# Shared-expert products and products of constants put into TensorE's waits

## The chip, the cores and the metric

One core of one Trainium2 chip runs the whole program in one launch. The metric is the device time of that launch in microseconds. Everything is float32.

## The reference, cut to what matters

Two layers (`DEPTH = 2`) of a diffusion backbone over 256 context and 256 latent tokens, width 1024. Layer 0 works on all 512 tokens (four tiles of 128), layer 1 writes only the 256 latent ones (two tiles).

```
for l in range(DEPTH):
    mod = silu(c) @ w_mod[l] + b_mod[l]
    h   = modulate(rms_norm(x), mod[0], mod[1])
    mix = gated delta rule | latent attention | windowed GQA | dense GQA of (h @ w_in[l])
    x   = x + mod[2] * (mix @ w_out[l])
    h   = modulate(rms_norm(x), mod[3], mod[4])
    x   = x + mod[5] * moe_ffn(h)

def moe_ffn(h):                      # 64 experts, 6 of them for each token
    scores = sigmoid(h @ router_w)
    idx    = top_k(scores + router_bias, 6)
    gates  = scores[idx] / sum(scores[idx]) * 2.5
    # assignments sorted by expert, each expert: swiglu of width 384
    return sum over k of gates[k] * swiglu(h, expert idx[k]) + swiglu(h, shared)
```

## The kernel before, in words

The engines run their own programs and meet at semaphores. A layer goes through stages. Input projections end with a barrier of all engines. The **delta rule** runs over four blocks (`b`) of 128 tokens in two directions (`d`): per block TensorE makes the decays (`decays`, L1153 and L1159) and the products of keys (`products`), then a long chain of small 64x64 products (`blocks`, L1142) in turn with ScalarE and VectorE. Its first block needs GpSimd's `X` (L2474) and then, for the step "n2", VectorE's transposed tile "NT" (L2081). Attention and the output projection (L1349) follow.

The **expert stage** starts with a sorting. Routing scores give a mask (VectorE, ends at L2272). TensorE sums it into positions (`positions`, L1380 and L1382). VectorE makes a key per expert, compares keys (`beats`, L2286), finds the first eight experts (`sorted_round(0)`, which releases the first weight loads, `sorted_ready` 1), then needs the ranks from TensorE (`ranks`, L1388; copied at L2311), and makes one-hot rows for slots (L2328) which TensorE multiplies into the lists by expert (`lists_by_expert`, L1394) and by unit (`lists_by_unit`, L1399). The finished lists (L2333 to L2336) release GpSimd's gathers of token rows (L2566). Then VectorE runs the seven other sorting rounds (L2290 to L2298); the last one gives `sorted_ready` 2, on which all later expert weights wait.

Work on tokens goes by units, n = 0, 1, 2, ... Units 0 and 1 (`EARLY = 2`) are two tiles of the shared expert, which need no gather and whose weights are loaded before the sorting; the others are routed experts, with the last shared tiles (layer 0 only) late among them. A unit is `unit_part(n, "lo")` and `unit_part(n, "hi")` (gate and up products, L1479, eight k-steps in two halves), SiLU on ScalarE (L1796), `unit_times` on VectorE (L2254), `act_transposed` (L1495, copied at L1802), `unit_down` (L1504), and copies out: ScalarE L1817 and VectorE L2260 (`shared_out`) or L2409. Routed tokens are transposed by `unit_transposed` (L1461) and copied by `unit_copied` (L2392, L2393).

Weights move in chunks of 1536 KB through a ring of eight slots (`SLOTS = 8`); the queue of SP issues them in the order of use (L890). The first three chunks are the shared expert's, the next five belong to units 2 and 3 and are the ones released by `sorted_ready` 1. Each later chunk waits until the chunk before it in its slot was used: after the lo half (`lo_used`), the hi half (`gu_psum`) or the down products (`down_psum`). For the ninth chunk and the two behind it these are unit 1's lo, hi and, in layer 0, down.

TensorE's order around the sorting is written out by hand, separately for `n_t == 4` (layer 0) and `n_t == 2` (layer 1):

```
layer 0: unit 0 hi | positions | act 0 | down 0 | ranks | unit 1 lo, hi | lists | act 1 | down 1 | unit 2 transposed
layer 1: unit 0 hi | positions | act 0 | down 0 | ranks | lists | unit 1 lo, hi | unit 2 transposed
```

After the units comes the **combining** (`combined`, one function per engine). Rows of expert outputs are read back by token (`yrow`, L934, 3072 KB a tile). GpSimd makes a diagonal of the gates (L2628, `diag_ready`), TensorE multiplies diagonals with rows (L1007; the trace shows each float32 product as two MATMULs, so a tile is 20 of them), VectorE adds and scales (L1920 to L1922, `resid_ready`). In layer 0 the next layer's norm follows tile by tile (VectorE L1905 to L1907, `normed_tile` on TensorE, L1021), then a barrier and the next layer's convolution projections (L1037). In layer 1 the output store follows and the program ends.

## Time and profile before

| what | value |
|---|---|
| time, median of 3 runs | 2623.26 us (2618.08 to 2626.28) |
| the profiled execution's own time | 2640.14 us |
| its span, first to last instruction | 2638.3 us, 41374 instructions |
| TensorE busy | 2256.7 us (86%), mean granted clock 0.944 |
| VectorE, ScalarE, GpSimd busy | 730.8 us (28%), 425.1 us (16%), 311.4 us (12%) |
| DMA queue of SP | 740.46 MB, 68.1% of 16 engines' span |
| expert weights | 256 + 128 loads of 1536 KB |

A timeline row gives the start, the length from first start to last end, engine, line, operation, output and inputs, one shape, the count, and in brackets the idle time before it with what ended it. The stages of layer 0 lie at about 196 to 305 us (delta rule), 544 to 594 (sorting), 594 to 1390 (units), 1396 to 1453 (combining and norm); those of layer 1 at 1586 to 1690, 1802 to 1840, 1840 to 2598 and 2603 to the end.

### The profile page before, as it was taken

The page shows a single profiled execution, that of the slowest core. Times are in us where ns is not written, and L with a number is a line of the kernel's source. Part 1 is how long each engine was busy: PE and PEld are TensorE (multiplying, and loading weights), DVE is VectorE, ACT ScalarE, POOL GpSimd, SP SyncE. Part 2 cuts the span into 40 slices and gives each one's busy share as a digit, 9 for nine tenths or more (in the row PEclk, how much of TensorE's full clock was granted, in tenths as well). Part 3 has the DMA queues.
Part 4 walks back from the last instruction along what each step waited for, and adds up shares of the span by engine and source line. Part 5 has one row for each costly group of instructions (what it writes and reads, how often), then busy time and mean ns, then how long its engine had stood idle before and what let it go on. Part 6 is the DMA issues. An engine that isn't in the chain of part 4 may idle for free. (4 is left out here: it accounts for less than half of the span.)

```text
span 2638.3 us, 41374 instructions
## 1 busy us (share of the span) xinstructions
PE 2256.7 (86%) x17495; PEld 1168.1 (44%) x17495; DVE 730.8 (28%) x1621; ACT 425.1 (16%) x886; POOL 311.4 (12%) x368
## 2 busy tenths in 40 slices
PE   6998899989877887888896998898978879888886
PEld 2457644454333343344443557755433334343332
DVE  3465554363101110111114365555211011111111
ACT  2323443210000000000001232441000000000000
POOL 0007200011111111110000006200111110000000
PEclk9999997999999999999998999999999999999998
DMA  7000286349999999999997010125999999999994
GB/s 321 32 18 33 102 356 262 127 163 389 426 422 416 410 416 421 410 421 398 381 397 324 33 41 19 70 101 218 351 426 418 413 417 420 420 415 416 414 421 182
DMA packets 96349, 780.99 MB, mean 296 GB/s; under 512 B 21736, under 2 KB 22136, under 8 KB 37280
## 3 DMA queue, kind: packets, MB, share of 16 engines
q1 hardware_dynamic: 74848, 740.46, 68.1%
q0 software_dynamic: 21312, 37.81, 3.8%
q8 instruction: 143, 2.34, 0.3%
q14 instruction: 46, 0.38, 0.0%
HBM read 772.55 MB, written 41.29 MB: 308 GB/s over the span
## 5 line engine op out<-in xcount | busy, mean ns | idle before, releaser
L1479 PE MATMUL banks<-arena,htreg 128*32 128x384 f32 (+2 forms) x5824 | 870.7, 529 | 218.0 <-DMA arena<-in_exp_w_gu 212.7
L1479 PEld LDWEIGHTS banks<-arena,htreg 128*32 128x32 f32 (+2 forms) x5824 | 401.5, 136 | 660.3 <-issue 511.3
L1504 PE MATMUL banks<-arena,modreg 128*32 128x512 f32 (+2 forms) x2184 | 398.2, 596 | 28.9 <-issue 25.5
L2254 DVE TENSOR_TENSOR modreg<-modreg,banks 128x384 f32<-128x384 f32 x74 | 41.0, 554 | 1044.3 <-ACT modreg L1796 1040.6
L1504 PEld LDWEIGHTS banks<-arena,modreg 128*32 128x32 f32 (+2 forms) x2184 | 134.2, 127 | 240.1 <-issue 236.3
L1049 PE MATMUL banks<-arena,htreg 128*128 128x512 f32 (+3 forms) x480 | 158.9, 490 | 0.0
L2409 DVE COPY modreg<-banks 128x512 f32<-128x512 f32 x68 | 47.0, 692 | 304.4 <-PE banks L1504 304.4
L1796 ACT ACTIVATE modreg<-banks 128x384 f32<-128x384 f32 x74 | 36.4, 492 | 541.7 <-PE banks L1479 541.7
L1802 ACT ACTIVATE modreg<-banks 128x384 f32<-128x384 f32 x74 | 36.3, 491 | 520.8 <-PE banks L1495 520.8
L2572 POOL DMA_INDIRECT y_d<-modreg,lst x68 | 67.5, 993 | 441.6 <-DVE modreg L2409 440.7
L1049 PEld LDWEIGHTS banks<-arena,htreg 128*128 128x128 f32 x480 | 89.6, 191 | 64.9 <-issue 60.9
L1817 ACT ACTIVATE modreg<-banks 128x512 f32<-128x512 f32 x68 | 40.6, 597 | 424.2 <-PE banks L1504 424.2
L2566 POOL DMA_INDIRECT htreg<-h_d,lsg x34 | 35.0, 1031 | 528.8 <-PE banks L1461 498.6
L2566 POOL DMA_INDIRECT hreg<-h_d,lsg x34 | 35.0, 1030 | 520.5 <-PE banks L1461 453.8
L1007 PE MATMUL banks<-arena 128*128 128x512 f32 x120 | 57.3, 638 | 31.6 <-DMA arena<-y_d 31.6
L1349 PE MATMUL banks<-arena,htreg 128*128 128x512 f32 x192 | 83.2, 593 | 0.0
L1304 PE MATMUL banks<-arena 64*128 64x512 f32 (+3 forms) x144 | 78.5, 630 | 2.6 <-ACT arena L1730 2.6
L1037 PE MATMUL banks<-htreg,arena 128*128 128x512 f32 (+1 forms) x192 | 78.7, 574 | 1.2 <-ACTq L703 0.7
L1142 PE MATMUL banks<-arena 64*64 64x64 f32 x1536 | 59.7, 226 | 7.5 <-DVE arena L2081 6.8
L1142 PEld LDWEIGHTS banks<-arena 64*64 64x64 f32 x1536 | 52.5, 140 | 15.4 <-DVE arena L2081 8.1
L959 PE MATMUL banks<-arena,crep 128*32 128x512 f32 x256 | 41.2, 733 | 20.2 <-DMA arena<-in_w_mod 20.2
L1314 PEld LDWEIGHTS banks<-const,htreg 128*128 128x128 f32 x240 | 28.4, 154 | 64.5 <-issue 42.4
(398 smaller groups left out, 2186.4 us busy)
## 6 DMA issues: line engine op xcount, KB each, us to landing
arena<-in_exp_w_gu SPq DMA_DIRECT2D x256, 1536.0 KB
arena<-in_exp_w_down SPq DMA_DIRECT2D x128, 1536.0 KB
arena<-in_w_mod SPq DMA_DIRECT2D x32, 1024.0 KB, 9.4
arena<-y_d SPq DMA_DIRECT2D x6, 3072.0 KB, 16.7
modreg<-in_w_mod SPq DMA_DIRECT2D x14, 1024.0 KB, 7.9
modreg<-mod_d SPq DMA_DIRECT2D x20, 512.0 KB
arena<-in_shared_w_gu SPq DMA_DIRECT2D x6, 1536.0 KB
arena<-in_w_in SPq DMA_DIRECT2D x4, 2048.0 KB, 12.9
```

The lines of the kernel that those rows point to most:

```text
L959: last = mm(bank[32 * c_:32 * c_ + 32, :], crep[:, k, :], w[:, 512 * c_:512 * c_ + 512], start=(k == 0), stop=(k == KD - 1))
L1007: last = mm(ps[4 + 2 * (i % 2) + half][:], diag[i % 2][:, k, :], yrow[i % YB][:, k, 512 * half:512 * half + 512], start=(k == 0), stop=(k ...
L1037: last = mm(qkv_bank(ct)[:, lo:], win_qkv[:, k, tok(ct)], hT[:, k, lo:], start=(i == 0), stop=(i == KD - 1))
L1049: last = mm(ps[2 + n % 4][:, lo:w], hT[:, k, tok(t)], win[g][:, k, lo:w], start=(k == 0), stop=(k == KD - 1))
L1142: last = mm(out[r, at + HALF * g:at + HALF * g + HALF], lhs(r, g), rhs(r, g), start=True, stop=True)
L1304: mm(ps[s % 2][:, 0:nk * P], q_, k_, start=True, stop=True).then_inc(scores_psum.sem, 1)
L1349: last = mm(ps[2 + n % 2][:], mixT[:, k, tok(t)], wout[:, k, 512 * half:512 * half + 512], start=(k == 0), stop=(k == KD - 1))
L1479: last = mm(gu_bank(n, half)[rows, 0:DE], src[:, k, rows], up4[q][:, i, DE * half:DE * (half + 1)], start=(k == 0), stop=(k == KD - 1))
L1504: last = mm(ps[4 + half][rows, :], actT[:, k, rows], dn3[q][:, k, 512 * half:512 * half + 512], start=(k == 0), stop=(k == KE - 1))
L2409: dve.tensor_copy(outs[r % 2][:, 512:1024], ps[5][:]).then_inc(unit_y.sem, 1)
L2566: pool.indirect_dma_start(out=slots[l][r % 2], out_offset=None, in_=h_d, in_offset=bass.IndirectOffsetOnAxis(ap=lsg1[:, u:u + 1], axis=0), ...
L2572: pool.indirect_dma_start(out=y_d, out_offset=bass.IndirectOffsetOnAxis(ap=lst1[:, u:u + 1], axis=0), in_=outs[r % 2], in_offset=None, bou ...
```

## The change

`keep_warm` multiplies the identity with 512 columns of constants into a bank that nothing reads; it is called in four places on TensorE. TensorE's order in the sorting becomes:

```
layer 0: unit 0 hi | unit 1 lo | positions | act 0 | ranks | down 0 | unit 1 hi | lists | act 1 | down 1 | unit 2 transposed
layer 1: unit 0 hi | positions | act 0 | down 0 | ranks | unit 1 lo | lists by expert, by unit | unit 1 hi | unit 2 transposed
```

On VectorE, in layer 0, `shared_out(0)` moves from ahead of the ranks, and `unit_times(1)` from behind the lists, to a place between the last one-hot row and the lists; `unit_copied(EARLY)` goes ahead of `shared_out(1)`. Nothing else changes.

```
@@ -949,6 +949,11 @@
         @block.tensor
         def _(pe):
             mm = pe.matmul
+
+            def keep_warm(bank, n):
+                for _ in range(n):
+                    mm(bank, ident, const[:, 0:512], start=True, stop=True)
+
             pe.wait_ge(ident_loaded.sem, 16)
             pe.wait_ge(cond_silu.sem, 1)
             pe.transpose(ps[4][:, 0:2 * KD], crow, ident[0:2 * KD, 0:2 * KD]).then_inc(first_psum.sem, 1)
@@ -999,6 +1004,8 @@
                 for i in range(NOUT[l] + 1):
                     if i < NOUT[l]:
                         pe.wait_ge(diag_ready.sem, diag_ready.at(l, i + 1))
+                        if i == 0:
+                            keep_warm(ps[4], 8)
                         pe.wait_ge(yrow_loaded[i % YB].sem, yrow_loaded[i % YB].at(l, i // YB + 1))
                         if i >= 2:
                             pe.wait_ge(resid_ready.sem, resid_ready.at(2 * l + 1, i - 1))
@@ -1007,6 +1014,9 @@
                                 last = mm(ps[4 + 2 * (i % 2) + half][:], diag[i % 2][:, k, :],
                                           yrow[i % YB][:, k, 512 * half:512 * half + 512], start=(k == 0), stop=(k == BY_PE - 1))
                             last.then_inc(out_psum.sem, 1)
+                    if i == NOUT[l] and l + 1 < DEPTH:
+                        pe.wait_ge(resid_ready.sem, resid_ready.at(2 * l + 1, i - 1))
+                        keep_warm(ps[4], 6)
                     if i and l + 1 < DEPTH:
                         normed_tile(2 * (l + 1), i - 1)
 
@@ -1180,8 +1190,10 @@
                                               start=True, stop=True)
                         pe_.done(last, l, b, "kk")
 
+                keep_warm(delta[0].C, 1)
                 decays(0)
                 products(0)
+                keep_warm(delta[0].C, 2)
                 both = list(zip((0, 1), delta, g_pe, g_act, g_dve, g_pool))
                 for b in range(NB):
                     for d, D_, pe_, act_d, dve_, pool_ in both:
@@ -1522,16 +1534,18 @@
                     act_transposed(0)
                     unit_down(0)
                     ranks()
+                    unit_part(1, "lo")
                     lists_by_expert()
                     lists_by_unit()
-                    unit_up(1)
+                    unit_part(1, "hi")
                     unit_transposed(EARLY)
                 else:
+                    unit_part(1, "lo")
                     positions()
                     act_transposed(0)
+                    ranks()
                     unit_down(0)
-                    ranks()
-                    unit_up(1)
+                    unit_part(1, "hi")
                     lists_by_expert()
                     lists_by_unit()
                     act_transposed(1)
@@ -2305,8 +2319,6 @@
                 link(ts(latecol[lo64], rankcol[lo64], float(NE - G_), -float(NE - U_), ALU.is_ge, ALU.mult))
                 link(ts(rankcol[lo64], rankcol[lo64], dropcol[lo64], latecol[lo64], ALU.add, ALU.add))
                 link(ts(unit_hot[lo64, 0:U_], K("experts")[lo64, 0:U_], rankcol[lo64], None, ALU.is_equal))
-                if n_t > 2:
-                    shared_out(0)
                 dve.wait_ge(rank_psum.sem, rank_psum.at(l, 1))
                 link(dve.tensor_copy(rank, ps[0][:, 0:NE]))
                 link(ts(shift_by, rank, float(U_), 2.0, ALU.is_ge, ALU.mult))
@@ -2329,6 +2341,9 @@
                        ).then_inc(slot_hot_ready.sem, 1)
                 dve.wait_ge(slot_hot_used.sem, slot_hot_used.at(l, TOPK * n_t))
                 dve.tensor_copy(listT, ps[1][lo64, 0:P]).then_inc(listT_ready.sem, 1)
+                if n_t > 2:
+                    shared_out(0)
+                    unit_times(1)
                 dve.wait_ge(list_psum.sem, list_psum.at(l, 1))
                 link(ts(row64[:, 0:U_], ps[0][:, 0:U_], 0.0, float(NO_CODE), ALU.is_equal, ALU.mult))
                 link(stt(row64[:, 0:U_], ps[0][:, 0:U_], -1.0, row64[:, 0:U_], ALU.add, ALU.add))
@@ -2336,8 +2351,6 @@
                 ts(lsg1[:, 0:U_], lst1[:, 0:U_], 3, None, ALU.logical_shift_right).then_inc(lists_ready.sem, 1)
                 if n_t == 2:
                     shared_out(0)
-                else:
-                    unit_times(1)
                 for j in range(1, NE // 8):
                     sorted_round(j)
                 if n_t == 2:
@@ -2392,11 +2405,9 @@
                     dve.tensor_copy(hgT[q % 2][:, 0:4, :], ps[0][:].rearrange("p (k n) -> p k n", k=4))
                     dve.tensor_copy(hgT[q % 2][:, 4:8, :], ps[1][:].rearrange("p (k n) -> p k n", k=4)).then_inc(slotT.sem, 1)
 
-                if n_t == 2:
-                    unit_copied(EARLY)
-                else:
+                unit_copied(EARLY)
+                if n_t > 2:
                     shared_out(1)
-                    unit_copied(EARLY)
                 gates_made()
                 def unit_out(n):
                     if is_shared(l, n):
```

## Rows read from the trace of the kernel before

**Rows 1.** Windows; columns: us, PE, PEld, DVE, ACT, POOL busy, PEclk, DMA share, GB/s.

```profile
580.00:590.00 10.00, 7.54 (x37) 4.46 (x37) 8.32 (x44) 0.49 (x1) 2.04 (x2) 1.00 0.51 182
...
640.00:700.00 60.00, 52.21 (x537) 21.69 (x539) 7.56 (x12) 4.74 (x9) 8.96 (x9) 0.97 1.01 426
...
1833.00:1890.00 57.00, 55.47 (x282) 29.79 (x281) 17.77 (x47) 4.63 (x9) 6.02 (x6) 1.00 0.82 300
```

**Rows 2.** Timeline of TensorE, layer 0's sorting; start us, us, what, xcount [idle before].

```profile
555.52 1.44 PE L1380 MATMUL banks<-arena,const 128*128 128x320 f32 x2 [3.96 <-DVE arena L2272]
556.75 2.45 PE L1382 MATMUL banks<-arena,const 128*128 128x256 f32 x8
...
566.19 10.59 PE L1479 MATMUL banks<-arena,htreg 128*128 128x384 f32 x32
576.70 6.17 PE L1394 MATMUL banks<-arena,modreg 128*64 128x128 f32 x48
...
586.36 5.39 PE L1504 MATMUL banks<-arena,modreg 128*128 128x512 f32 x12 [0.67 <-ACT modreg L1802]
...
594.01 10.59 PE L1479 MATMUL banks<-arena,htreg 128*128 128x384 f32 x32 [1.38 <-DVE htreg L2393]
```

**Rows 3.** Timeline of VectorE, the same stretch.

```profile
560.72 0.25 DVE L2286 TENSOR_SCALAR stat<-arena,stat 64x64 f32<-64x64 f32 x1
...
565.99 0.69 DVE L2260 COPY hreg<-banks 128x512 f32<-128x512 f32 x1 [2.78 <-PE banks L1504]
566.60 0.21 DVE L2311 COPY arena<-banks 128x64 f32<-128x64 f32 x1
...
574.18 1.11 DVE L2328 TENSOR_SCALAR arena<-const,arena 128x128 f32<-128x128 f32 x4
```

**Rows 4.** Timeline of the weight loads' queue, the same stretch.

```profile
592.27 7.68 SPq L890 DMA_DIRECT2D arena<-in_exp_w_gu  x4
```

**Rows 5.** Timeline of TensorE, layer 1's sorting.

```profile
1820.79 5.38 PE L1394 MATMUL banks<-arena,modreg 128*64 128x128 f32 x24 [5.34 <-DVE arena L2328]
...
1826.98 10.59 PE L1479 MATMUL banks<-arena,htreg 128*128 128x384 f32 x32
...
1839.99 5.43 PE L1479 MATMUL banks<-arena,htreg 128*128 128x384 f32 x16 [1.53 <-DVE htreg L2393]
```

**Rows 6.** Timeline of GpSimd, layer 1's first gather.

```profile
1828.80 1.08 POOL L2566 DMA_INDIRECT hreg<-h_d,lsg  x1 [66.41 <-DVE lsg L2336]
```

**Rows 7.** Timeline of GpSimd, the diagonals of layers 0 and 1.

```profile
1396.50 2.47 POOL L2628 TENSOR_TENSOR arena<-const,gate 128x640 f32<-128x640 f32 x2 [4.01 <-issue]
...
2602.96 2.47 POOL L2628 TENSOR_TENSOR arena<-const,gate 128x640 f32<-128x640 f32 x2 [2.90 <-issue]
```

**Rows 8.** Timeline of TensorE, both combining stages and what follows layer 0's.

```profile
1406.38 19.38 PE L1007 MATMUL banks<-arena 128*128 128x512 f32 x40 [16.39 <-DMA arena<-y_d]
...
1453.49 1.97 PE L1021 MATMUL banks<-const,hreg 128*128 128x128 f32 x8 [7.24 <-DVE hreg L1907]
...
1456.17 37.29 PE L1037 MATMUL banks<-htreg,arena 128*128 128x256 f32 x96 [0.72 <-ACTq L703]
...
2612.82 20.32 PE L1007 MATMUL banks<-arena 128*128 128x512 f32 x40 [15.25 <-DMA arena<-y_d]
```

**Rows 9.** Windows while the combining starts, columns as in rows 1.

```profile
1410.00:1412.00 2.00, 2.00 (x6) 0.97 (x5) 0.00 (x0) 0.00 (x0) 0.00 (x0) 0.91 1.14 492
...
2618.00:2620.00 2.00, 2.00 (x5) 0.91 (x4) 0.00 (x0) 0.00 (x0) 0.00 (x0) 0.83 0.46 197
```

**Rows 10.** Timeline of TensorE, first delta block of layers 0 and 1.

```profile
206.59 1.15 PE L1142 MATMUL banks<-arena 64*64 64x64 f32 x32 [2.52 <-DVE arena L2081]
...
213.27 1.08 PE L1153 MATMUL banks<-arena,const 128*64 128x256 f32 x8
...
1593.96 1.40 PE L1142 MATMUL banks<-arena 64*64 64x64 f32 x32 [2.36 <-DVE arena L2081]
...
1602.19 1.08 PE L1153 MATMUL banks<-arena,const 128*64 128x256 f32 x8
```

31 lines of the change are left out of this document (20 added, 11 removed).

## The prediction

> **What bounds the kernel now.** I read the windows of the page's slices first, then the timelines of each engine around the places that the change touches. The windows show two kinds of stretches. While units run, the DMA engines are full: share 1.01 at 426 GB/s with TensorE busy for 52 of 60 us [rows 1]. The expert weights set the pace there, and a change in that stretch would bring nothing. Ahead of it DMA is not full: share 0.51 in the last part of layer 0's sorting, and still 0.82 over the first 57 us of units in layer 1, where TensorE is busy 55.5 of 57 us and hands back slots of the ring too late [rows 1]. So what counts is when the stream of weights becomes continuous, and what starts it earlier moves everything behind it. Two things start it: the last sorting round, on which the ninth chunk waits (issued at 592.27 [rows 4]), and the start of unit 2, whose halves free further slots (594.01 [rows 2] and 1839.99 [rows 5]).
>
> **Term A, layer 0's sorting.** TensorE stands idle for 3.96 us up to 555.52, waiting for the mask [rows 2]. Unit 1's lo half, 16 MATMULs of the 32 that take 10.59, so 5.3 us [rows 2], now runs from 551.6 to 556.8. That makes positions start 1.3 later. But they ran at the low clock: 10 MATMULs from 555.52 to 559.20, 3.7 us, for 1920 columns in all; the pace of unit 1 (10.59 for 32 x 384 columns, 0.86 ns a column [rows 2]) gives 1.65, and with 0.4 for ends 2.05. Behind an unbroken run I expect the high clock, so positions end at 558.85, 0.35 earlier than before. If the clock fell anyway they would end 1.3 later.
> Next, ranks needs VectorE's comparison, before complete at 560.97 [rows 3], now 560.6. It no longer stands behind unit 0's down products. Before, VectorE waited 2.78 us for these (until 565.99), copied their output for 0.69, and took the ranks at 566.60 [rows 3]. Now it reaches them at 565.99 - 2.78 - 0.3 = 562.9, 3.7 earlier, and its first one-hot row moves from 574.18 [rows 3] to 570.5. TensorE does ranks until 561.0, down 0 in 5.3 until 566.3, and hi in 5.3 until 571.6. So the lists start at 571.6 instead of 576.70 [rows 2], 5.1 earlier; TensorE is what is late here, and VectorE's one-hot rows stand ready.
> Behind the last one-hot row VectorE now does the shared copy (0.69) and unit 1's product (0.55 by the same columns); about 0.5 of that lies in its wait for the lists by unit, and the product was ahead of the seven rounds before as well. The ninth chunk moves by 5.1 + 0.5 - 0.7 = 4.9, to 587.4. Down 1 was at 586.36 [rows 2]; its input is ready at 579.3, with transpose and copy it starts near 580.6 and ends at 585.9. It frees a slot ahead of 587.4. Unit 2's transposes follow, then VectorE's two copies (1.3), and unit 2 starts at 588.2, 5.8 earlier. Slots that unit 2 frees come 5.8 earlier, the first chunk 4.9: I take **5.3**. Bounds: 3.5, if the positions are 1.3 late and VectorE's added work of 1.2 shows in full (5.3 - 1.6 - 0.2), and 5.8.
>
> **Term B, layer 1's sorting.** Here ranks stays where it was. TensorE sits idle for 5.34 us ahead of 1820.79, in which the clock falls: 24 MATMULs of the lists take 5.38 (0.224 each), against 48 in 6.17 (0.129 each) in layer 0 [rows 2, 5]. Unit 1's lo half, 5.3, fits into the 5.34. It delays nothing, and the lists then take 12 x 0.257 = 3.1: 2.3 gained. Only hi remains behind them (TensorE was busy with both halves for 10.59 from 1826.98 [rows 5]), so it ends at 1824.6 + 5.3 = 1829.8 instead of 1837.5. What is late next is the gather of unit 2's rows: it was issued at 1828.80 [rows 6], now 1826.5. How long it takes cannot be read, since it was covered; it is under 1837.4 - 1828.8 = 8.6. The other late part is VectorE: seven rounds from 1826.2, some 6.1 us, unit 1's product, then the two copies. With about 5 for the gather both sides meet near 1832.5 to 1833, and unit 2 starts at 1834.4, against 1839.99 [rows 5]: 5.6. With 8.6 for the gather it starts at 1837.5: 2.5. The ninth chunk itself moves only 2.3, but DMA has 0.18 x 57 = 10 us of slack in the stretch [rows 1], so unit 2's start counts. I take **5.3**, bounds 2.3 and 5.9.
> The Trainium skill, "DMA: Bandwidth & Descriptors", section "Anatomy of one DMA", gives a fixed 2.0 us for a DMA of GpSimd plus its bytes at 436 GB/s. For 512 KB that would be 3.2 us by an estimate from this page, the gather would be there before the hi half ends, and term B would be about 5.8.
>
> **Term C, 8 constant products ahead of each combining.** Each is two MATMULs of 512 columns: 0.44 us at the pace of rows 2, 0.88 at half clock. Their room is from the first diagonal (1396.50 + 1.25 and 2602.96 + 1.25 [rows 7]) to the rows' arrival (1406.38 and 2612.82 [rows 8]): 8.6 us in both layers. Queued behind them are the combining products, and behind those VectorE. The clock rose 4.0 us after the first product in layer 0 (share at the high level in the window from 1410) and 5.9 after it in layer 1 [rows 8, 9]. So 16 MATMULs take between 9.0 (4.6 cold, 11.4 warm) and 10.0 (6.7 cold, 9.3 warm), mean 9.5: 0.9 late. What they save: 40 MATMULs took 19.38 and 20.32 [rows 8] against 40 x 0.44 = 17.6, so 1.8 and 2.7. Net **0.9** and **1.8**. Bounds: 0.4 to 1.4 and 1.3 to 2.3, and -5.5 each if the clock stayed low throughout (16 x 0.88 = 14.1 in 8.6).
>
> **Term D, 6 constant products ahead of layer 0's last tile.** TensorE is idle 7.24 us there [rows 8]; 12 x 0.44 = 5.3 fit in. The wait on the residual that is added ahead of them is for tile 2, which VectorE has done by then. The eight transposes take 1.97 and would take half, and the 96 MATMULs behind them take 37.29 [rows 8] for 80 x 0.44 = 35.2 at full clock. Together **3.0** if the clock holds over the remaining 2 us of idle time, 0 if it does not.
>
> **Term E, constants in the delta rule.** One product ahead of the first decays costs 0.9 in a wait of 1.7 for GpSimd: nothing. Two products, 1.8 us, lie in the waits of 2.52 (layer 0) and 2.36 (layer 1) [rows 10], nothing. In layer 0 the clock held; from first product to the next block's decays took 213.27 - 206.59 = 6.7. In layer 1 it took 1602.19 - 1593.96 = 8.2 [rows 10]. Gain **1.5** in layer 1, bounds 0 and 1.5. Were a cover gone, 1.8 a layer would show.
>
> **Sum.** 5.3 + 5.3 + 0.9 + 1.8 + 3.0 + 1.5 = 17.8 us. The profiled execution took 2640.1 (span 2638.3), 16.9 above the median of 2623.3; I take the same 17.8 off the median: **2605.5 us**. The Trainium skill, "TensorE: Matmul & The Clock Gate", section "Part 1: The HAM clock gate", says that the number of cold products varies from run to run of one kernel. By that, terms C to E would differ between executions within the bounds above, and the sum with them.
>
> **The rivals.** (1) The forecast, 0.66. (2) The early start is partly given back: the gather, and VectorE's rounds behind it, hold unit 2 back in both layers, and one of D and E fails. 3.5 + 2.3 + 2.7 + 3.0 = 11.5, 2612. For it: the gather's time isn't seen. Against it: layer 0's gather is issued 4.9 ahead of its use, and the rounds end before it. 0.17. (3) The stream does not begin earlier in effect: later slots are freed by units whose pace is set elsewhere, and DMA's slack closes. Only C, D and E remain, 7.2: 2616. For it: in layer 1 DMA reaches full share only after some 50 us. Against it: TensorE is without pause there, so an earlier start has to carry through. 0.09. (4) The clock doesn't rise during constant products, as if the change did not do what it says: C gives -11, D and E nothing, A and B 9.3 (A without the positions' gain 4.0): 2625. Against it: products of this shape raise it in both layers [rows 9]. 0.04. (5) Slower: the gathers and chunks now overlap more, and the weight stream loses rate. 302 MB a layer at 426 GB/s take 709 us, so 1% costs 7.1 a layer; from 1.8% in both layers it decides (25.6), at 2.3% it gives 2605.5 + 32.6 = 2638. For it: layer 1's first 57 us show only 300 GB/s [rows 1]; against it: these are waits for slots, not a low rate. 0.04.
>
> **Numbers.** A measurement of this kernel can tell about 0.3%, 7.9 us, from no change. Faster by more: (1) and nearly all of (2), 0.82. Within: (3), (4) and the rest, 0.14. Slower 0.04. The upper bounds sum to 5.8 + 5.9 + 1.4 + 2.3 + 3.0 + 1.5 = 19.9, and 5 more for the spread of the three runs: 2598. The other end takes in (2) and half of (3): 2616.
>
> **What would show it.** Right: the lists of layer 0 start about 5 us after TensorE's mask wait than before relative to it, that is 20 instead of 25 us after unit 0's hi half; the ninth chunk is issued 4.9 earlier, unit 2 of layer 1 starts 5.6 earlier against ranks; the 40 combining MATMULs take 17.6 and start about 0.9 behind their rows; clock 1.00 at L1037 and after L1142's first product. Wrong: a new wait for a gather at L1461, a wait of TensorE for weights in the first units, or a weight stream that ends no earlier although it began earlier.

## The result, and the profile after

| | time | ratio to the kernel before, 95% interval |
|---|---|---|
| kernel after | 2609.25 us (2605.43 to 2622.77, 14 runs) | 0.9934 (0.9919 to 0.995) |
| kernel before, beside it | 2626.78 us (2618.08 to 2633.53, 14 runs) | |
| kernel after, timed again with later experiments | 2611.6 us (2605.08 to 2622.28, 6 runs) | 0.9937 (0.9915 to 0.9958) |

17.5 us less, where 17.8 were forecast. The profiled execution of after took 2607.57 us (span 2605.8). The two profiled spans differ by 32.5 us, which is more than the medians do. 10.4 of it lie between the delta rule's last decays and unit 0's hi half of layer 0, in attention, which the change does not touch. That stretch alone took between 261 and 281 us in the fourteen profiled executions of this study. So spans of whole executions are not compared here; stages are. Below, a row or tile is called cold where it ran at the low clock. Lines of a kernel shift with each edit; L955 is the products of constants.

Layer 0's sorting on TensorE (rows 2 has the same stretch of before; columns: start us, length, engine, line, operation, output and inputs, count, idle time before it and what ended it):

```profile
535.58 10.59 PE L1491 MATMUL banks<-arena,htreg 128*128 128x384 f32 x32
546.00 0.70 PE L1392 MATMUL banks<-arena,const 128*128 128x320 f32 x2
546.54 1.31 PE L1394 MATMUL banks<-arena,const 128*128 128x256 f32 x8
...
549.68 0.43 PE L1400 MATMUL banks<-stat,const 64*128 64x64 f32 x2 [1.45 <-DVE stat L2300]
550.04 5.42 PE L1516 MATMUL banks<-arena,modreg 128*128 128x512 f32 x12
555.29 5.33 PE L1491 MATMUL banks<-arena,htreg 128*128 128x384 f32 x16
560.55 6.17 PE L1406 MATMUL banks<-arena,modreg 128*64 128x128 f32 x48
...
569.45 7.08 PE L1516 MATMUL banks<-arena,modreg 128*128 128x512 f32 x12 [0.67 <-ACT modreg L1816]
...
578.87 10.59 PE L1491 MATMUL banks<-arena,htreg 128*128 128x384 f32 x32 [1.45 <-DVE htreg L2406]
```

Positions and the idle time ahead of them read as forecast: no wait for the mask, 0.70 and 1.31 us at full clock instead of 1.44 and 2.45 [rows 2]. Lists start 25.0 us behind the start of unit 0's hi half, before 30.6 (19.6 and 25.1 behind its end, where the prediction had 20 and 25). New is the length of unit 1's down products, 7.08 us for the 12 MATMULs that took 5.39 [rows 2]. SP issued the ninth chunk at 576.11 (40.5 us behind the hi half, before 46.1), and the windows of after say what happened to the clock while the down products ran (columns: busy us and count of each engine, granted clock, DMA share, GB/s):

```profile
576.11 1.37 SPq L890 DMA_DIRECT2D arena<-in_exp_w_gu  x3
```

```profile
570.00:572.00 2.00, 2.00 (x4) 0.76 (x3) 1.79 (x12) 0.00 (x0) 1.69 (x2) 0.61 1.00 334
572.00:574.00 2.00, 2.00 (x4) 0.93 (x3) 1.76 (x12) 0.00 (x0) 0.03 (x1) 0.54 0.84 277
```

Behind the lists' small products and three waits of 0.38 to 0.67 us the granted clock is 0.61 and 0.54, in the middle of large products with TensorE busy throughout. The same rows and waits left it at 1.00 in another execution (e1 below), so they do not explain the fall by themselves.

Layer 1's sorting, TensorE and GpSimd of after (against rows 5 and 6):

```profile
1787.87 5.43 PE L1491 MATMUL banks<-arena,htreg 128*128 128x384 f32 x16
1793.28 3.25 PE L1406 MATMUL banks<-arena,modreg 128*64 128x128 f32 x24
...
1797.24 5.43 PE L1491 MATMUL banks<-arena,htreg 128*128 128x384 f32 x16
1805.60 1.68 PE L1473 MATMUL banks<-const,hreg 128*128 128x128 f32 x8 [2.93 <-DMA hreg<-h_d,lsg]
1808.66 7.51 PE L1491 MATMUL banks<-arena,htreg 128*128 128x384 f32 x16 [1.38 <-DVE htreg L2406]
```

```profile
1799.06 1.08 POOL L2577 DMA_INDIRECT hreg<-h_d,lsg  x1 [64.20 <-DVE lsg L2351]
```

The lists take 3.25 instead of 5.38 us, as forecast. Then TensorE waits 2.93 us for the gather, which took 6.5 us from its issue. The wait costs a second time: the granted clock is still 1.00 from 1804 to 1806, then 0.51 and 0.50 up to 1812, and unit 2's first half takes 7.51 us instead of 5.4.

Combining, the last tile's constants and transposes, the projections (L1047) and the delta rule of layer 1, TensorE (against rows 8 and 10):

```profile
1381.18 9.62 PE L955 MATMUL banks<-const 128*128 128x512 f32 x16 [7.78 <-POOL arena L2639]
1390.64 17.33 PE L1014 MATMUL banks<-arena 128*128 128x512 f32 x40
...
1410.13 8.82 PE L1014 MATMUL banks<-arena 128*128 128x512 f32 x20 [1.29 <-POOL arena L2639]
...
1429.12 5.32 PE L955 MATMUL banks<-const 128*128 128x512 f32 x12
1435.69 1.09 PE L1031 MATMUL banks<-const,hreg 128*128 128x128 f32 x8 [1.25 <-DVE hreg L1921]
1437.56 36.24 PE L1047 MATMUL banks<-htreg,arena 128*128 128x256 f32 x96 [0.77 <-ACTq L703]
```

```profile
1572.43 1.15 PE L1152 MATMUL banks<-arena 64*64 64x64 f32 x32 [0.53 <-DVE arena L2095]
...
1579.11 1.08 PE L1163 MATMUL banks<-arena,const 128*64 128x256 f32 x8
...
2583.13 17.43 PE L1014 MATMUL banks<-arena 128*128 128x512 f32 x40 [0.57 <-DMA arena<-y_d]
```

40 combining MATMULs take 17.33 and 17.43 us instead of 19.38 and 20.32. In layer 0 the constants end behind their rows (no idle time ahead of the combining), in layer 1 0.57 us before them. TensorE's third tile starts within 0.1 us of the landing of its own rows in both kernels, 30.1 and 30.3 us behind the first diagonal; what reaches the projections goes through VectorE, whose adding of the second tile starts 1.2 us earlier behind the first diagonal.

Stage by stage, in us, for all profiled executions. *hi-u2*: unit 0's hi half to unit 2's start in layer 0. *u2-dg*: on to the first diagonal. *dg-pr*: on to the projections L1047. *pr-dc*: on to layer 1's first decays. *dc*: on to the next block's decays. *dc-rk*: on to the ranks. *rk-u2*, *u2-dg*, *dg-end*: the same for layer 1, from its ranks to unit 2, to the first diagonal and to the end.

```
                          hi-u2  u2-dg  dg-pr  pr-dc    dc  dc-rk  rk-u2  u2-dg  dg-end
before                     47.9  802.5   59.7  131.1  14.9  212.8   25.0  763.0    35.3
e11_combining_constants    51.6  802.4   58.3  128.6  15.7  209.9   24.9  762.7    32.9
e10_delta_constants        48.5  802.9   59.4  129.4  13.4  209.2   24.9  763.3    35.0
e2_constants_only          51.0  803.2   57.8  128.2  13.4  208.4   25.0  761.9    33.5
e4_layer1_order            51.4  800.1   59.3  129.4  15.8  209.9   21.1  763.9    35.1
e3_layer0_order            44.8  802.4   59.8  131.1  14.9  213.0   24.9  761.9    34.2
e5_copy_before_ranks       47.6  800.1   59.5  131.0  14.9  213.2   24.9  763.0    35.2
e1_order_only              41.6  801.9   59.7  131.3  14.9  213.0   21.6  765.1    34.2
after                      43.3  801.0   57.7  128.1  13.4  208.4   21.2  763.5    33.7
e17_after_again            43.3  802.9   58.1  128.4  13.4  207.9   20.9  764.8    33.4
e14_six                    43.3  803.1   58.9  126.8  13.4  208.1   20.7  764.1    33.6
e15_last_chunk             43.3  801.2   57.6  131.3  13.4  208.0   19.1  764.9    33.5
e12_five_more              41.7  802.4   57.9  128.5  13.4  211.1   21.0  763.3    32.9
e16_rounds                 41.7  805.1   58.3  129.2  13.4  208.4   20.6  762.9    33.1
```

### The profile page after: what moved, and what is told of

Its sections match the earlier page's. It is cut to its first block and busy times, and to the rows that moved or that the text cites. A ratio compares the mean times of both kernels' runs of the same rounds, so it can differ in the third digit from the quotient of the medians.

```text
span 2605.8 us, 41483 instructions
## 1 busy us (share of the span) xinstructions
PE 2265.0 (87%) x17551; PEld 1163.8 (45%) x17551; DVE 729.3 (28%) x1621; ACT 423.8 (16%) x886; POOL 311.1 (12%) x368
## 5 line engine op out<-in xcount | busy, mean ns | idle before, releaser
L1059 PEld LDWEIGHTS banks<-arena,htreg 128*128 128x128 f32 x480 | 89.4, 190 | 64.6 <-issue 60.7
L1047 PE MATMUL banks<-htreg,arena 128*128 128x512 f32 (+1 forms) x192 | 77.7, 568 | 1.2 <-ACTq L703 0.8
L1316 PE MATMUL banks<-arena 64*128 64x512 f32 (+3 forms) x144 | 71.3, 577 | 3.3 <-ACT arena L1744 3.3
L1361 PEld LDWEIGHTS banks<-arena,htreg 128*128 128x128 f32 x192 | 36.2, 190 | 44.0 <-issue 44.0
L1047 PEld LDWEIGHTS banks<-htreg,arena 128*128 128x128 f32 x192 | 37.5, 196 | 40.2 <-issue 37.2
```

Source lines behind the costliest of these rows:

```text
L1047: last = mm(qkv_bank(ct)[:, lo:], win_qkv[:, k, tok(ct)], hT[:, k, lo:], start=(i == 0), stop=(i == KD - 1))
L1059: last = mm(ps[2 + n % 4][:, lo:w], hT[:, k, tok(t)], win[g][:, k, lo:w], start=(k == 0), stop=(k == KD - 1))
L1316: mm(ps[s % 2][:, 0:nk * P], q_, k_, start=True, stop=True).then_inc(scores_psum.sem, 1)
L1361: last = mm(ps[2 + n % 2][:], mixT[:, k, tok(t)], wout[:, k, 512 * half:512 * half + 512], start=(k == 0), stop=(k == KD - 1))
```

## The experiments

My theory was the forecast's: orders (A, B) and constants (C, D, E) each give their part. The rivals: it is all one of the two, or the weight stream takes the early start back. A gain in us below is the ratio's distance from 1 times 2630 us. The medians give somewhat other gains: 12.1 us for e1, 10.8 for e2, 10.1 for e3, 4.3 for e4, 4.6 for e10, 20.6 for e12.

### Orders alone and constants alone

e1_order_only deletes the four sets of constants, e2_constants_only keeps them and puts back both sorting orders and VectorE's steps.

```
e1:  -                        if i == 0:
     -                            keep_warm(ps[4], 8)
     ...
     -                keep_warm(delta[0].C, 2)
e2:  -                    unit_part(1, "lo")
                          positions()
                          act_transposed(0)
     -                    ranks()
                          unit_down(0)
     -                    unit_part(1, "hi")
     +                    ranks()
     +                    unit_up(1)
     ...
```

> All constant products are taken out; both new orders of the sorting and VectorE's moved steps stay. Theory (the forecast's terms A and B are real, C to E come on top): 8.4 to 10.6 us faster than the kernel before (8.4 by the stage lengths of the two profiled executions, 4.6 in layer 0 and 3.8 in layer 1; 10.6 by the forecast), so about 0.9965 of it, and the combining again takes 19 to 20 us for its 40 MATMULs. Rival (the whole gain is clock, the earlier start of the weight stream is lost again in the units): within 3 us of the kernel before, with unit 2 to the diagonal longer by what the sorting won. Rival (only the orders count): 15 us or more faster.

> The four sets of constant products alone, on the orders of before. Theory: 6 to 8 us faster than the kernel before: combining 1 in layer 0 and 1.8 in layer 1, last tile and decays 3, layer 1's delta rule 1.5; with e1_order_only's gain it sums to the whole 17.5. Rival (only the orders count): within 2 us of the kernel before. Rival (the clock, kept higher at these places, also avoids the low stretches elsewhere): over 10 us faster, and more in stretches without a constant product.

Measured beside each other: e1 2617.87 us, ratio 0.9951 (0.9931 to 0.9971), 12.9 us faster (0.0049 x 2630). e2 2619.16 us, 0.9964 (0.9944 to 0.9983), 9.5 us faster. e1 is not within 3 us of before and e2 is not within 2 us, so both rivals of the kind "only one counts" fall. Together they make 22.4, against the 17.5 of the whole; each has an interval of about 5 us to both sides, which holds the difference. The combining of e1 took 19.58 and 19.27 us, as expected. The time does not exclude e2's last rival, over 10 us with a gain in stretches without a constant, and the stages bear it out in part: *dc-rk* has no constant in it and was 4.4 us shorter than in before.

### One layer's order at a time

e3_layer0_order_only is e1 with layer 1's order put back, e4_layer1_order_only is e1 with layer 0's.

```
e3:  -                    unit_part(1, "lo")        e4: as in the diff of e2,
                          lists_by_expert()             TensorE and VectorE of layer 0
                          lists_by_unit()
     -                    unit_part(1, "hi")
     +                    unit_up(1)
```

> Layer 0's order of TensorE and VectorE alone; no constant product, layer 1 as before. Theory: 4.6 us faster by the stage lengths (5.3 by the forecast): ninth chunk 5 to 5.6 us earlier against unit 0's hi half, unit 2 4.6 to 5.8 earlier, all of it carried to the diagonal. Down 1 again takes about 7 us and not 5.4, if the clock falls behind the small products of the lists. Rival (stream gives it back): under 2 us, and layer 0's units longer by the same amount.

> Layer 1's order of TensorE alone (unit 1's lo half between ranks and lists). Theory: 3.8 us faster by the stage lengths (5.3 by the forecast), with TensorE idle about 3 us for the gather of unit 2's rows ahead of its transposes, and the gather landing about 6.5 us after its issue. Rival (DMA's slack in layer 1's first units closes and only the ninth chunk counts): 2.3 us or less, units of layer 1 longer by the rest. Sum of e3 and e4 should be e1 within 2 us.

Measured: e3 2619.85 us, 0.9975 (0.9956 to 0.9994), 6.6 us faster. e4 2625.63 us, 0.9994 (0.9977 to 1.0011), 1.6 us faster, not to be told from nothing. Their sum is 8.2, e1 had 12.9; each has intervals of 5, so the 2 us that I had expected them to agree within could not be tested. Nor do the times exclude the rivals, under 2 us for e3 and 2.3 or less for e4; for e3 the stages do, since *u2-dg* (802.4) is that of before.

The stages say more than the times. In layer 0 the way to unit 2 depends on whether the clock falls in the two sets of down products. TensorE of e1, and of e3:

```profile
545.60 5.42 PE L1509 MATMUL banks<-arena,modreg 128*128 128x512 f32 x12
...
565.01 5.39 PE L1509 MATMUL banks<-arena,modreg 128*128 128x512 f32 x12 [0.67 <-ACT modreg L1809]
```

```profile
543.81 7.11 PE L1509 MATMUL banks<-arena,modreg 128*128 128x512 f32 x12
...
564.92 6.91 PE L1509 MATMUL banks<-arena,modreg 128*128 128x512 f32 x12 [0.67 <-ACT modreg L1808]
```

5.4 and 5.4 us in e1, 7.1 and 6.9 in e3, of the same code. The old order has both cases too: 5.39 twice in before and e10, 7.0 to 7.4 twice in e2, e4 and e11. So like must be held against like: with both sets at full clock 41.6 (e1) against 47.9 and 48.5 (before, e10), 6.3 and 6.9 less; with the fall in both 44.8 (e3) against 51.0, 51.4 and 51.6, 6.1 to 6.8 less. **Layer 0's order is worth 6.1 to 6.9 us** at unit 2's start, and the profiled pair showed 4.6 only because the clock fell in one set of after and in none of before.

In layer 1 the offsets to before, measured from the ranks, tell where the gain stays (start of each unit, in us against the same start in before):

```
unit        e3      after     e1      e12     e15     e16
2         -0.06    -3.81   -3.36   -3.93   -5.88   -4.32
3         -0.07    -1.76   -1.55   -3.94   -4.22   -4.32
6         -0.06    -1.75   -1.55   -3.94   -4.22   -4.32
8         -0.76    -2.97   -1.19   -4.26   -5.03   -4.19
20        -1.09    -3.41   -0.89   -3.67   -3.66   -3.85
35        -1.11    -3.32   -1.29   -3.58   -3.91   -4.42
```

In after unit 2 starts 3.8 us earlier, and unit 3 only 1.8: the 2.05 between are unit 2's cold first half (7.51 against 5.43). It is constant from there to unit 6, while TensorE alone sets the pace. Behind that the offsets move by 1 us and more, also in e3, which has layer 1 as before. In after the gain grows again, to 3.3 us at unit 35, so the 2.05 us lost ahead of unit 3 are not all missing at the end; e12 and e15, 2.2 and 2.5 us ahead of after at unit 3, are 0.3 and 0.6 ahead at unit 35.

At the first diagonal, counted from the ranks, the six executions with layer 1's old order have 786.8 to 788.2 us, mean 787.6, and the five that have the new order and no further change of layer 1's units (e1, e4, after, e14, e17) 784.7 to 786.7, mean 785.4. So **layer 1's order is worth about 2.2 us there**, with a spread of 1 us between executions of one kernel. e1, at 786.7, shows almost nothing of it.

### VectorE's part in layer 0

e5_layer0_copy_before_ranks takes e3 and puts the copy back ahead of the ranks:

```
+                if n_t > 2:
+                    shared_out(0)
                 dve.wait_ge(rank_psum.sem, rank_psum.at(l, 1))
...
                 if n_t > 2:
-                    shared_out(0)
                     unit_times(1)
```

> e3_layer0_order_only with one step put back: in layer 0 VectorE copies unit 0's down products before it takes the ranks, as in the kernel before; TensorE's order stays new. Theory (the ranks taken ahead of the copy are what lets the lists start early): VectorE waits for down 0 until about 20 us after unit 0's hi half and reaches its first one-hot row 7.6 us behind the ranks' copy, so TensorE's lists start 3 us later than in e3_layer0_order_only (about 28 to 29.5 us after unit 0's hi half instead of 25 to 26.7), TensorE waits for them, and unit 2 starts about 3 us later. Rival (TensorE alone is late, VectorE's order costs nothing): lists and unit 2 as in e3_layer0_order_only within 0.5 us.

Measured, one execution: 2624.69 us. VectorE and TensorE of e5:

```profile
555.29 0.69 DVE L2266 COPY hreg<-banks 128x512 f32<-128x512 f32 x1 [5.38 <-PE banks L1509]
```

```profile
563.88 7.54 PE L1399 MATMUL banks<-arena,modreg 128*64 128x128 f32 x48 [3.52 <-DVE arena L2334]
```

VectorE waits 5.38 us for the down products, and TensorE then waits 3.52 for VectorE's one-hot rows. The lists come 30.3 us behind unit 0's hi half, 5.3 later than in e1 and 3.6 later than in e3, and the rival falls. Its way to unit 2 (47.6) looks like that of before (47.9), but the two are not alike: in e5 the first down products took 7.11 us and the lists 7.54 instead of 6.2, the second down products 5.39. Against e3, with the 1.5 us that e3's second down products lost to the clock added, the copy's old place costs about 4.3 us, an estimate from one execution each. By the same reckoning (49.2 against 51.0 to 51.6) TensorE's new order alone still brings about 2 us, so VectorE's move is most of what layer 0's order is worth, and not all of it.

### What the constants do further on

In after and e2, with all constants, *dc-rk* was 208.4 us, in before, e1 and e3 212.8 to 213.0, and no constant product stands in this stretch. e10 keeps only the delta rule's three products, e11 only those at the combining.

```
e10: -                            keep_warm(ps[4], 8)      e11: -                keep_warm(delta[0].C, 1)
     -                        keep_warm(ps[4], 6)               -                keep_warm(delta[0].C, 2)
     (both: orders as in e2)
```

> Only the three constant products of the delta rule, everything else as before. Open: in the kernel after and in e2_constants_only the way from layer 1's second decays to its ranks took 208.4 us, in the kernel before, e1 and e3 212.9, with no constant product in it. Theory F (the delta rule's constants keep the clock in block 2 and leave it so that the two later low stretches do not fall): 208.4 us here too, and 13.4 instead of 14.9 between the first decays, 6 us faster than before in all. Rival G (the combining's constants, which only shift all later work against the clock's falls, do it): 212.9 us here, 1.5 us faster in all.

> Only the constant products ahead of the combining in both layers and ahead of layer 0's last tile. Theory F of e10_delta_constants_only: 212.9 us from layer 1's second decays to its ranks. Rival G: 208.4 us. Either way the diagonals to L1047's place is 2.0 us shorter and the way from there to the decays 2.9 shorter, and the end comes 1.7 us earlier against layer 1's first diagonal.

Measured: e10 2624.71 us, 0.9992 (0.9971 to 1.0013), an interval that holds both the 6 us of F and the 1.5 us of G; e11 2621.33 us in one execution. *dc-rk* was 209.2 in e10 and 209.9 in e11, and e4, without a constant, had 209.9 as well. Neither F nor G is right as put, and e4 shows that the stretch varies by 3 us by itself. Between before and after, two stretches of low clock differ (the first windows of 20 us are of before, the next of after, at the same places behind the second decays):

```profile
1602.20:1622.20 20.00, 17.49 (x460) 15.37 (x460) 11.57 (x31) 5.12 (x11) 11.96 (x18) 0.91 0.01 2
1702.20:1722.20 20.00, 19.21 (x145) 11.31 (x146) 9.69 (x29) 11.03 (x24) 0.00 (x0) 0.83 0.23 95
```

```profile
1579.10:1599.10 20.00, 17.49 (x514) 15.36 (x512) 12.00 (x32) 5.75 (x12) 13.50 (x21) 1.00 0.01 3
1679.10:1699.10 20.00, 18.70 (x183) 11.27 (x182) 12.48 (x40) 11.92 (x30) 0.00 (x0) 1.00 0.12 52
```

Six of seven executions with both kinds of constants had 207.9 to 208.4 (the seventh 211.1), four of five with neither had 212.8 to 213.2 (the fifth 209.9). The constants go with some 4 us here; by what path stays open. *dc* is plain: 13.4 in all eight with the delta rule's constants, 14.9 to 15.8 in all six without. Layer 0's first block, where the prediction saw nothing to gain, shows it too: from its first decays to the next block's it took 16.0 us in all eight, and in the six without 15.9 in three and 17.1 to 18.7 in the other three (e1, e3, e11).

### More constants

e12_five_more_constants fills three more waits of after:

```
 layer 1: unit_part(1, "hi")           layer 0: act_transposed(0)         layer 0: lists_by_unit()
         +keep_warm(ps[6], 3)                  +keep_warm(ps[6], 1)               +keep_warm(ps[6], 1)
          unit_transposed(EARLY)                ranks()                            act_transposed(1)
```

> The kernel after plus five more constant products: one ahead of layer 0's ranks (in the 1.45 us wait for VectorE), one ahead of the transposes for unit 1's down products, three in layer 1 between unit 1's hi half and the transposes of unit 2, where TensorE waits 2.9 us for the gather. Theory: the clock holds, unit 0's and unit 1's down products take 5.4 us each instead of up to 7.1, unit 2 of layer 0 starts 41.6 to 42.2 us after unit 0's hi half (43.3 in the kernel after), transposes in layer 1 take 1.05 instead of 1.7 and unit 2's lo half 5.4 instead of 7.5; 3 to 4 us faster than the kernel after, 20 to 22 faster than before. Rival: the added products only lengthen the path (0.9 us in layer 0) and the clock falls all the same: 0 to 1 us slower than the kernel after.

TensorE of e12, layer 0 and layer 1:

```profile
563.35 1.02 PE L955 MATMUL banks<-const 128*128 128x512 f32 x2
...
565.33 5.42 PE L1516 MATMUL banks<-arena,modreg 128*128 128x512 f32 x12
...
582.72 1.12 PE L955 MATMUL banks<-const 128*128 128x512 f32 x2
...
584.86 5.39 PE L1516 MATMUL banks<-arena,modreg 128*128 128x512 f32 x12 [0.67 <-ACT modreg L1819]
...
1820.91 2.74 PE L955 MATMUL banks<-const 128*128 128x512 f32 x6
1824.41 1.16 PE L1473 MATMUL banks<-const,hreg 128*128 128x128 f32 x8 [0.77 <-DMA hreg<-h_d,lsg]
1826.95 5.43 PE L1491 MATMUL banks<-arena,htreg 128*128 128x384 f32 x16 [1.38 <-DVE htreg L2409]
```

The stages came as expected: 41.7 us to unit 2 in layer 0, both sets of down products at 5.4, and in layer 1 unit 3 keeps 3.94 instead of 1.76 us. The time was 2608.71 us, 0.9902 (0.9878 to 0.9925), 25.8 us faster than before by the ratio and 20.6 by the medians. Against after's 0.9934 and 0.9937 the intervals overlap, so 3 to 4 us over after fit, but are not shown by the times. In layer 1 little of it reaches the first diagonal: 784.4 us behind the ranks, where after had 784.6, e14 784.8 and e17 785.7.

### The gather, and the number of constants

e15_last_chunk_after_gather holds one weight chunk back, e14_six_before_combining takes two products away.

```
e15: +                    if l == 1 and loaded == 7:
     +                        sp.wait_ge(gathered[0].sem, gathered[0].at(l, 1))
e14: -                            keep_warm(ps[4], 8)
     +                            keep_warm(ps[4], 6)
```

> The kernel after with one more wait on SP: in layer 1 the fifth of the chunks issued together (the last before the ninth chunk's round) is issued only when unit 2's rows are gathered. In the kernel after the gather was issued at 1799.06 and landed about 6.5 us later, with the DMA engines at share 1.0 for the first 4 of them. Theory (the gather is slow because it shares the DMA engines with the weight chunks issued ahead of it): 3 to 4 us from issue to landing, TensorE's wait ahead of unit 2's transposes falls from 2.9 us to under 1, the clock stays, and unit 2 starts 18 to 19 us behind ranks instead of 21.2. Rival (6.5 us is the gather's own time, or that of the scattered rows): the wait stays at about 2.9 us and unit 2 starts at 21.2 us. The units of layer 1 take no more than 1 us longer in either case.

> The kernel after with 6 instead of 8 constant products ahead of each combining. In layer 0 the 8 held the combining back by 0.9 us after its rows had come (the 16 MATMULs take 9.1 to 9.6 us, cold at first), in layer 1 they ended 0.6 us before. Theory: 12 MATMULs take 7.4 to 7.9 us, combining in layer 0 begins with its rows, 9.9 us behind the first diagonal instead of 10.8, and its 40 MATMULs still take 17.4 us, so 0.9 us gained in layer 0, nothing in layer 1. Rival (the clock falls again in the 1 to 1.5 us of idle time between them and the combining, or has not risen in one of the layers): the 40 MATMULs take 18.5 us or more in that layer, so slower than with 8.

GpSimd and TensorE of e15:

```profile
1802.65 1.08 POOL L2579 DMA_INDIRECT hreg<-h_d,lsg  x1 [64.20 <-DVE lsg L2353]
```

```profile
1807.16 1.16 PE L1475 MATMUL banks<-const,hreg 128*128 128x128 f32 x8 [0.90 <-DMA hreg<-h_d,lsg]
1810.19 7.10 PE L1493 MATMUL banks<-arena,htreg 128*128 128x384 f32 x16 [1.86 <-DVE htreg L2408]
```

4.5 us from issue to landing instead of 6.5 (6.5 to 7.0 in the seven executions with this order and no chunk held back), and TensorE's wait falls from 2.93 to 0.90: at least 2 us of the gather's time are spent behind the chunks. What the remaining 4.5 us are, with four chunks issued ahead, stays open; the theory had 3 to 4. Unit 2 starts 19.1 us behind the ranks, just outside the expected 18 to 19, but the clock still fell (7.10 us), against the theory, and of the 2.1 us won, 0.6 were left at the first diagonal (19.1 + 764.9 against 21.2 + 763.5), less than the 1.1 us between after and e17. One execution each: e15 2610.41 us, e14 2610.69, before beside them 2621.48.

e14's combining began with its rows, 10.0 us behind the first diagonal. But TensorE, being earlier, waited longer for the rows of the third tile, which landed 30.4 us behind the first diagonal, and that tile ran cold:

```profile
1393.22 17.43 PE L1014 MATMUL banks<-arena 128*128 128x512 f32 x40 [0.60 <-DMA arena<-y_d]
...
1413.64 10.52 PE L1014 MATMUL banks<-arena 128*128 128x512 f32 x20 [2.12 <-issue]
```

10.52 us for 20 MATMULs instead of 8.82, and 58.9 us from the diagonal to the projections instead of 57.7: slower in this stage, though by neither way that I had named. VectorE had been 0.6 us ahead of after, and then waited 1.62 us for the cold tile. The length of the wait alone does not decide: in e12 the same tile waited 2.20 us and ran at full clock, in 8.82 us. So what 6 products bring when the third tile stays fast is open.

The stage behind it gave the loss back: 126.8 us from the projections to the decays, after 128.1. The projections themselves took 34.64 us instead of 36.24, and their first 4 us ran at 1.00 in e14 (first fence) and at 0.59 in after (second):

```profile
1440.23 1.09 PE L1031 MATMUL banks<-const,hreg 128*128 128x128 f32 x8 [0.59 <-DVE hreg L1921]
1442.10 34.64 PE L1047 MATMUL banks<-htreg,arena 128*128 128x256 f32 x96 [0.77 <-ACTq L703]
...
1442.10:1446.10 4.00, 4.00 (x19) 3.54 (x20) 0.00 (x0) 0.16 (x1) 0.17 (x2) 1.00 0.52 164
```

```profile
1437.56:1441.56 4.00, 4.00 (x11) 3.29 (x12) 0.00 (x0) 0.00 (x0) 0.17 (x2) 0.59 0.49 164
```

All eight executions with these constants fall into two groups by the wait between the constants ahead of the last tile and its transposes. With 0.59, 0.59 and 0.83 us (e14, e12, e16) L1047 took 34.64; with 1.25 to 2.10 us (after, e15, e2, e11, e17) it took 36.20 to 36.33. In the six without constants, behind 7.24 us or more, it took 37.1 to 37.4. So 6 products were too few in after: the wait that they left, with the 0.77 us behind the transposes, went with a fall of the clock. No run varied this number by itself.

### Unit 2 or the ninth chunk

e15 and e12 left open which of the two sets layer 1's end. e16_rounds_in_ranks_wait moves the ninth chunk alone; e17_after_again is after, unchanged.

```
+                early = 4 if n_t == 2 else 1
+                for j in range(1, early):
+                    sorted_round(j)
                 dve.wait_ge(rank_psum.sem, rank_psum.at(l, 1))
...
-                for j in range(1, NE // 8):
+                for j in range(early, NE // 8):
```

> e12_five_more_constants with VectorE's sorting rounds 1 to 3 of layer 1 moved ahead of its 3.4 us wait for the ranks (four rounds stay behind the lists). Theory N (in layer 1 the ninth chunk's issue, not unit 2's start, sets when the weight stream ends): ninth chunk 15.9 us behind ranks instead of 18.6, unit 2's start unchanged at about 21.0, and from ranks to layer 1's first diagonal 781.7 us instead of 784.4, so 2.7 us faster than e12_five_more_constants and about 6 faster than the kernel after. Rival U (unit 2's start sets it, as the forecast had it): ranks to the first diagonal stays at 784.4. Rival Q (the ninth chunk, issued while the gather is under way, slows the gather further): unit 2 starts 1 to 3 us later and the gain is under 1 us.

> The kernel after, unchanged, timed beside e16_rounds_in_ranks_wait and for the spread between executions: 16 to 19 us faster than the kernel before. If terms depend on where the clock falls, layer 0's unit 0 hi half to unit 2 lies between 41.6 and 43.3 us and the way from layer 1's second decays to ranks between 208 and 211 us again.

The ninth chunk was issued 15.8 us behind the ranks instead of 18.6, unit 2 started at 20.6, and the first diagonal came 783.5 us behind the ranks, against 784.4 in e12 and 784.6 in after. Theory N had 781.7, rival U 784.4: N is off by 1.8 and U by 0.9, and two executions of after differ by 1.1, so the run speaks for U without settling it. Rival Q falls: unit 2 started 0.4 us earlier than in e12, not later. e16 2609.2 us, 0.9938 (0.9915 to 0.9961); e17 2611.6 us, 0.9937. e17's ranges held but for *dc-rk*, 207.9. No version is measurably faster than after; e12 and e16 are ahead of it by 1.6 us in layer 0's way to unit 2 and by 2 at unit 3 in layer 1, of which 0.3 and 1.1 are left at the first diagonal; that is below what these runs can tell.

## Why the prediction was right, and where it was off

The sum was right (17.8 against 17.5) and so were the mechanisms of its terms, but for the wait for the gather in term B and the clock in term D; several sizes were off, and some errors cancelled.

- **What bounds the kernel.** Right in layer 0: rival 3, a stream that begins no earlier in effect, and rival 5, one that loses rate, fall there, since *u2-dg* is 800.1 to 803.2 in the five executions with the old order and 800.1 to 803.1 in eight of the nine with the new one (805.1 in e16). In layer 1 *u2-dg* is 761.9 to 763.3 with the old order and 763.5 to 765.1 in the five with the new order alone, 1.6 us more in the mean: a part of the early start is given back, mostly in unit 2's cold first half.
- **Term A**, 5.3, was too small by about 1: 6.1 to 6.9 for the order. TensorE's steps came as worked out (lists 5.6 earlier, forecast 5.1). The step that failed is the closing choice of 5.3 between the ninth chunk and unit 2. Both moved more (5.6 and 6.3 in e1, which like before had full clock in both sets of down products). VectorE's move is about two thirds of it (e5). What the term did not have is the clock in the down products: 1.5 to 2.0 us for each of two sets, in some executions and not in others.
- **Term B**, 5.3, was too large: 3.8 at unit 2's start, 1.8 behind its first half, and 3.3 at the first diagonal in the profiled pair, 2.2 there over all executions. The step that failed is "with about 5 for the gather", a number taken inside the bound of 8.6; it took 6.5, and 4.5 with one chunk held back. And the wait for it brought a cost that was not in the sum, 2.1 us of cold products. Rival 2 named the gather, and in layer 1 it happened: at unit 3, and in the mean at the first diagonal, the gain is below the forecast's lower bound of 2.3. The choice of unit 2 over the ninth chunk is not settled: e16 moved the chunk by 2.75 and gained 0.8 over e12, which speaks for it; but the chunk moved by 2.2 us in after as well (18.6 against 20.8 behind the ranks), which is the mean gain at the first diagonal.
- The estimate from the Trainium skill, "DMA: Bandwidth & Descriptors", "Anatomy of one DMA" (2.0 us fixed and the bytes at 436 GB/s, 3.2 us for 512 KB), is not met here: 6.5 us behind the chunks, 4.5 us with one of them held back. By it term B would have been 5.8, farther off.
- **Term C**, 0.9 and 1.8: measured 1.15 (0.9 late, 2.05 saved) and 1.75 (1.14 later, 2.89 saved). Right; in layer 0 it arrives through VectorE, which the term had behind the combining, while TensorE's third tile waits for its rows in either kernel.
- **Term D**, 3.0: measured 1.9 (transposes 0.88 shorter, L1047 1.05). The step that failed is that the clock holds over the rest of the idle time: L1047 began at 0.59 behind waits of 1.25 and 0.77 us and took 36.24. Where the first wait was 0.59 to 0.83 (e12, e14, e16) the clock held and L1047 took 34.64, near the term's 35.2, and the term is 3.5. The transposes behind 1.25 us of idle time were at full speed, as forecast.
- **Term E**, 1.5: measured 1.46, in every execution with the constants and in none without. Right; that layer 0 had nothing to gain was so in before, and not in e1, e3 and e11, which lost 1.2 to 2.8 us there without constants.
- **Not in the sum**: the stretch from layer 1's second decays to the ranks, some 4 us shorter with all constants. The profiled pair alone does not account for 17.5: from unit 0's hi half of layer 0 to the end its stages differ by 22.0 us, of which the terms as measured there are 4.6 + 1.8 + 1.15 + 1.75 + 1.9 + 1.5 = 12.7 and this stretch 4.4.
- **The sum, from all executions**, an estimate from the table's means: order of layer 0 6.5, order of layer 1 2.2; constants 1.6 (*dg-pr*, e14 left out), 1.9 (*pr-dc*), 1.8 (*dc*), 3.8 (*dc-rk*) and 1.5 (*dg-end*), 10.6 together. The constants agree with e2 (9.5); the whole, 19.3, lies inside after's interval (13.1 to 21.3). Against the forecast the orders brought 8.7 instead of 10.6, and the constants 10.6 instead of 7.2, of which 3.8 come from a stretch that no term named. I count the forecast's agreement in size as partly luck.
- The Trainium skill, "TensorE: Matmul & The Clock Gate", "Part 1: The HAM clock gate", says that the number of cold products varies from run to run of one kernel. The trace agrees, by more than I had allowed: identical down products took 5.4 or 7.1 us (e1, e3), and attention of layer 0 took 261 to 281 us, with stretches at 0.50 that differ between before and after (below).

## What to carry to other kernels

An idle engine can cost twice where its clock falls behind the wait: fill the wait with work that is due anyway, then with constants where nothing is left, up to its end (behind 0.59 to 0.83 us left over L1047 ran at full clock, behind 1.25 us it did not), and check that the other engine's order (here VectorE's copy ahead of the ranks) doesn't hold the result back. When a wait is filled or removed, price the transfer that becomes late next from its issue to its landing under the load of that moment, not from its size. To judge a change of some microseconds, compare stages that had the same clock: one profiled pair gave 4.6 us for a step that is worth 6.1 to 6.9. And follow a gain to the place where it counts: in layer 1 it was 3.8 us at unit 2, 1.8 at unit 3 and about 2.2 at the first diagonal.

## What the runs showed of the hardware that I had not expected

- A gather of 512 KB issued while five weight chunks were under way took 6.5 us, with DMA at share 1.02 while it was issued:

```profile
1798.00:1800.00 2.00, 2.00 (x8) 1.21 (x7) 1.84 (x10) 0.00 (x0) 0.94 (x1) 1.00 1.02 436
```

- The clock can be low for tens of microseconds while TensorE is busy throughout. In before's attention (the first two rows) it stayed at 0.50 with TensorE busy 10.00 of 10 us; in after (the other two) the clock had risen again within the first of the same windows, 0.79, and was at 1.00 in the second. What sets this off was not looked into.

```profile
440.00:450.00 10.00, 10.00 (x63) 5.60 (x56) 4.28 (x14) 3.27 (x9) 0.00 (x0) 0.50 0.78 305
450.00:460.00 10.00, 10.00 (x49) 5.17 (x48) 3.62 (x13) 3.37 (x9) 0.00 (x0) 0.50 0.35 145
```

```profile
440.00:450.00 10.00, 10.00 (x77) 5.02 (x76) 5.66 (x18) 3.63 (x10) 0.00 (x0) 0.79 0.72 282
450.00:460.00 10.00, 9.04 (x85) 5.29 (x84) 5.84 (x20) 6.14 (x18) 0.00 (x0) 1.00 0.40 168
```

- The clock can fall in the middle of large products, and not in every execution. After's 48 list MATMULs ran at 1.00, and the fall between 570 and 574 came behind three waits of 0.38 to 0.67 us. With the new order and the same three waits it came in after, e3, e14, e15 and e17, and not in e1. With two MATMULs of constants behind the second lists (e12, e16) it did not come in either execution, which is too few to show that the constants prevent it.
- Where the wait behind the constants was 0.59 to 0.83 us, L1047 ran at full clock from its start in three of three executions; behind 1.25 to 2.10 us it began low in five of five. At the third tile of the combining, 2.12 us of waiting went with a low clock in e14 and 2.20 us with full clock in e12.
